# Expert token lists from the positions of maxima, and 16-row output products in four column groups

## The chip, the cores and the metric

The kernel runs on one core of one Trainium2 chip. The metric is the device time of one execution in microseconds (us), as the median of several. Engines are called PE (TensorE), PEld (its weight loads), DVE (VectorE), ACT (ScalarE), POOL (GpSimd) and SP (SyncE, which issues most transfers). Everything is computed in f32, where one matrix product is two records on PE.

## The reference, cut to what matters

Two hybrid attention layers on 512 tokens and 16 meta tokens, then a second block on 512 latent tokens and 256 context tokens with a neighbourhood-attention mixer and an RWKV mixer, each followed by an expert layer. The parts that the change touches:

```python
mixed = jnp.concatenate([o_a * silu(dz), o_b * silu(fz)], axis=-1)
return h + jnp.einsum('blm,md->bld', mixed, w_out)      # hybrid layer, 528 rows
...
cap = EC_CAPACITY * T // N_EXPERTS                       # 64 latent, 32 context tokens
aff = softmax(h @ w_router)                              # T x 16
gate, idx = lax.top_k(aff.T, cap)                        # each expert picks its tokens
xin = h[idx]
hid = silu(xin @ w1) * (xin @ w3)                        # 1024 x 1024 per expert
y = (hid @ w2) * gate[..., None]
return segment_sum(y, idx)
```

The order of the tokens within an expert's list doesn't matter, since the results are added back by index.

## The kernel before, in words

The program is a chain of stages. Each stage gives every engine its own list of instructions, joined by semaphores, and ends with a barrier of all engines. The weights come in chunks of 2 MB (2,097,152 bytes). `load_chunk` (line 92) issues one on SP's queue into a slot, `chunk_here` (106) makes PE wait for it. There are three slots (`ring`); in the last expert stage four more are made out of buffers that are free by then (`WIDE_SLOTS`, 7). A slot is loaded again when PE has finished with its chunk. So in the first expert stage SP's loads follow the semaphores `up` and `down` of PE with two chunks in flight or waiting while PE works on the third, and in the second stage with six.

**Output projection of a hybrid layer** (`hybrid_output`, line 934). A job is one tile of rows by one half of 512 columns. `begin` (line 957) multiplies the four blocks of the forget half, `end` (line 966) the four of the differential half, and DVE adds the bank onto X (line 1012). Tiles are four of 128 rows and, in layer 0 only, one of 16 meta rows. Six jobs begin ahead (j = 0 to 5, the first meta job is j = 4); the last job of all, j = 9, is the second meta job. In `hybrid_project` the 16 meta rows already are multiplied in four groups of 128 columns, each written to its own 32 partitions (lines 436 to 438).

**Routing** (`route`, line 1577). Affinities are turned to 16 rows (experts) by tokens in `left` (latent at partition 0, context at partition 32). Then eight turns of `max` (eight largest of each row, line 1672) and `match_replace` (those eight become -1, line 1673) mark the 64 chosen tokens of each expert (context rows take part in the first four turns). A compare, a running sum, a product and a subtraction (lines 1674 to 1677) give every chosen token its place in the list; PE turns these back to tokens by experts (1632), and DVE copies them to `slot` (1681). The stage ends there.

**Experts** (`experts`, line 1685). For every expert, DVE builds a one-hot matrix out of `slot` (`choose`, 1871 to 1874), PE multiplies it by pairs of (token number, affinity) (`place`, 1792), and DVE copies the result to the list of indices and gates (`list_tokens`, 1883 and 1884). Token numbers and the comparison row come from HBM as `moe_labels` (1728). POOL gathers the rows of the expert (`gather`, 1752), two experts ahead, and adds the results into HBM (`scatter`, 1761). PE's order for one expert is: four chunks of w1 and w3 (`rows_by`, 1782), `place` for the expert two ahead, the transposes of the hidden rows (`flip_hid`, 1805), the transposes of the next expert's gathered rows (`flip_xin`, 1798), two chunks of w2. DVE and ACT run their part in a loop of 4 by 4 experts (`Fori`), PE's is written out. The last turns list and gather an expert that doesn't exist (index 16). The first stage has both streams (64 + 32 rows, six tiles), the second only the latent one.

```python
for r in streams:
    last = rows_by(xinT[:, x % 2], w, j % 2, r, r.gates if j // 2 else r.ups)
last.then_inc(s.up, 1)
...
pe.wait_ge(s.onehot, e + 3)
place(x % 2)
for r in streams:
    pe.wait_ge(s.hid_ready, e * NS + r.at + 1)
    flip_hid(r)
pe.wait_ge(s.listed, e + 3)
...
flip_xin((x + 1) % 2)
```

Of the kernel before, what the change touches and what calls it, by code (L numbers as in the profile page):

```python
# [933 lines left out]
def hybrid_output(k, l, O, OT, Z, squares, blocks, uT, tiles, held):  # L934
# [5 lines left out]
    BANKS_OUT = 6  # L940
    with ExitStack() as mem, stage(k, "rooted inverted gated turned back product added mod_turned mod_back") as (block, s):
# [8 lines left out]
        def _(pe):  # L950
            def begin(j):
                n, t, rows = jobs[j]
                w = chunk_here(k, pe, c0 + n)
                if j >= BANKS_OUT:
                    pe.wait_ge(s.added, j - BANKS_OUT + 1)
                for a in range(half):
                    nc.tensor.matmul(bank(k, j % BANKS_OUT)[0:rows, :], OT(a)[:, t * P:t * P + rows], w[:, half + a, :],
                                     start=a == 0, stop=False)

            def end(j):  # L960
# [4 lines left out]
                for a in range(half):  # L965
                    last = nc.tensor.matmul(bank(k, j % BANKS_OUT)[0:rows, :], uT[:, a, t * P:t * P + rows], w[:, a, :],
                                            start=False, stop=a == half - 1)
# [32 lines left out]
        def _(dve):  # L1000
# [7 lines left out]
            def add(j):  # L1008
# [3 lines left out]
                nc.vector.tensor_tensor(x, x, bank(k, j % BANKS_OUT)[0:rows, :], ALU.add).then_inc(s.added, 1)  # L1012
# [544 lines left out]
ROUND = 4  # L1557
HALF_K = KD // 2
EPAD = EXPERTS + ROUND
# [17 lines left out]
def route(k, l, hT, xn, sums, aff, slot, tiles):  # L1577
# [8 lines left out]
    with ExitStack() as mem, stage(k, "parts copied logits exped turned placed step ready") as (block, s):  # L1586
        sb = lambda n, shape: mem.enter_context(nc.sbuf_tensor(f"{n}{k.stage_no}", shape, F32))
        stat = sb("stat", [P, 2, 8])
        left, rank, ones = sb("left", [rows, SEQ]), sb("rank", [rows, SEQ]), sb("ones", [rows, SEQ])
        part, pick = sb("part", [P, TOK2]), sb("pick", [P, 2, EXPERTS])  # L1590
        best = sb("best", [rows, 8])
# [17 lines left out]
        def _(pe):  # L1609
# [24 lines left out]
            last.then_inc(s.placed, 1)  # L1634

        @block.scalar
        def _(act):
# [4 lines left out]
            act.wait_ge(s.step, 9)  # L1642
# [3 lines left out]
        def _(dve):  # L1646
# [19 lines left out]
            nc.vector.tensor_tensor(aff[:, 0:nt, 0:EXPERTS], raw[:, :, :], wide(stat[:, 1, 0:nt]), ALU.mult).then_inc(s.ready, 1)  # L1666
# [11 lines left out]
            dve.wait_ge(s.placed, 1)  # L1678
            for n, (_, first, width, _) in enumerate(streams):
                ts = slice(first // P, (first + width) // P)  # L1680
                chain(nc.vector.tensor_copy(slot[:, ts, 0:EXPERTS], bank(k, 5 + n, nt * EXPERTS)
                                            .rearrange("p (t e) -> p t e", t=nt)[:, ts, :]))
# [1543 lines left out]
```

## Time and profile before

| | us |
|---|---|
| median of 3 runs | 3560.84 (3553.47 to 3570.84) |
| the profiled execution | 3576.05 |
| its span, first to last instruction | 3574.3 |
| PE busy in the span | 3179.9 (89%) |
| DVE busy | 1522.1 (43%) |
| ACT busy | 828.7 (23%) |
| mean DMA rate over the span | 169 GB/s |
| share of transfers in the chain that ended last | 10% |

A row of the view by stretches gives the stretch in us from the span's start, its length, busy time of each engine with its number of instructions, the granted clock of PE (1 is full), the mean busy share of the 16 DMA engines and their rate. The stages that the change touches lie at 414 to 490 us (output projection of layer 0), 1467 to 2094 (first routing and experts) and 3027 to 3574 (second routing and experts).

### The profile page before, as it was taken

The page shows a single profiled execution, that of the slowest core. Times are in us where ns is not written, and L with a number is a line of the kernel's source. Part 1 is how long each engine was busy: PE and PEld are TensorE (multiplying, and loading weights), DVE is VectorE, ACT ScalarE, POOL GpSimd, SP SyncE. Part 2 cuts the span into 40 slices and gives each one's busy share as a digit, 9 for nine tenths or more (in the row PEclk, how much of TensorE's full clock was granted, in tenths as well). Part 3 has the DMA queues.
Part 4 walks back from the last instruction along what each step waited for, and adds up shares of the span by engine and source line. Part 5 has one row for each costly group of instructions (what it writes and reads, how often), then busy time and mean ns, then how long its engine had stood idle before and what let it go on. Part 6 is the DMA issues. An engine that isn't in the chain of part 4 may idle for free. (4 is left out here: it accounts for less than half of the span.)

```text
span 3574.3 us, 73074 instructions
## 1 busy us (share of the span) xinstructions
PE 3179.9 (89%) x32020; PEld 1830.5 (51%) x32020; DVE 1522.1 (43%) x3460; ACT 828.7 (23%) x1876; POOL 285.1 (8%) x307
## 2 busy tenths in 40 slices
PE   6998999989799999599999979998888878787777
PEld 5855658556344565344444435547788764322222
DVE  3574535645202483412122244137878863311111
ACT  2113410134201372100000010137666640000000
POOL 0001000000000120000000000001222230000000
PEclk9998999989899999799999989989999999899999
DMA  5564135720221111299999961100000033799998
GB/s 175 152 196 148 25 81 152 211 78 25 96 65 47 29 39 71 105 367 370 366 357 373 372 222 71 41 1 4 4 4 5 4 115 137 289 403 401 402 404 341
DMA packets 148488, 603.35 MB, mean 169 GB/s; under 512 B 17489, under 2 KB 20369, under 8 KB 131665
## 3 DMA queue, kind: packets, MB, share of 16 engines
q1 hardware_dynamic: 141840, 577.10, 43.9%
q0 software_dynamic: 6336, 21.63, 2.6%
q8 instruction: 253, 4.15, 0.5%
q14 instruction: 59, 0.48, 0.0%
HBM read 576.01 MB, written 28.97 MB: 169 GB/s over the span
## 5 line engine op out<-in xcount | busy, mean ns | idle before, releaser
L1782 PE MATMUL psum<-ring,big 128*32 128x256 f32 (+1 forms) x5280 | 692.8, 479 | 40.0 <-DMA ring<-moe_w 18.9
L1782 PEld LDWEIGHTS psum<-ring,big 128*32 128x32 f32 (+1 forms) x5280 | 242.3, 122 | 478.2 <-issue 383.3
L414 PE MATMUL psum<-h_uT,ring 128*128 128x264 f32 x1280 | 290.5, 387 | 0.0
L1920 DVE TENSOR_TENSOR big<-big,psum 128x512 f32<-128x512 f32 (+1 forms) x48 | 27.3, 597 | 613.0 <-PE psum L1782 613.0
L543 DVE SCALAR_TENSOR_TENSOR h_O<-h_O,cond_silu 128x512 f32<-128x512 f32 x336 | 226.8, 743 | 102.1 <-DMA h_O<-ada_w 102.1
L414 PEld LDWEIGHTS psum<-h_uT,ring 128*128 128x128 f32 x1280 | 242.0, 190 | 46.5 <-issue 5.8
L1782 PE MATMUL psum<-big 128*64 128x512 f32 x864 | 205.6, 622 | 54.7 <-DMA big<-moe_w 34.2
L1272 PE MATMUL psum<-ring,big 128*128 128x512 f32 x576 | 252.4, 598 | 1.7 <-PEq L56 1.7
L2391 PE MATMUL psum<-ring,gates 64*64 64x128 f32 (+1 forms) x5120 | 171.9, 253 | 11.5 <-issue 9.9
L1932 DVE SCALAR_TENSOR_TENSOR big<-psum,big,gates 64x512 f32<-64x512 f32 (+1 forms) x128 | 78.8, 615 | 241.4 <-PE psum L1782 240.0
L1272 PEld LDWEIGHTS psum<-ring,big 128*128 128x128 f32 x576 | 109.5, 192 | 135.3 <-issue 135.3
L434 PE MATMUL psum<-ring,h_uT 128*128 128x512 f32 x384 | 170.0, 600 | 0.0
L1782 PEld LDWEIGHTS psum<-big 128*64 128x64 f32 x864 | 62.0, 142 | 190.0 <-issue 128.2
L1859 ACT ACTIVATE big<-psum 128x512 f32<-128x512 f32 (+1 forms) x48 | 23.5, 524 | 579.2 <-PE psum L1782 579.2
L1058 PE MATMUL psum<-ring,big 128*128 128x512 f32 x320 | 139.5, 598 | 5.8 <-PEq L56 5.8
L2391 PEld LDWEIGHTS psum<-ring,gates 64*64 64x64 f32 x5120 | 134.8, 134 | 14.9 <-issue 13.7
L2739 DVE TENSOR_TENSOR ring<-ring,psum 64x256 f32<-64x256 f32 x288 | 120.9, 420 | 13.6 <-ACT ring L2576 7.8
L2391 PE MATMUL psum<-gates,ring 64*64 64x64 f32 x3840 | 88.3, 224 | 38.8 <-ACT ring L2576 34.0
L434 PEld LDWEIGHTS psum<-ring,h_uT 128*128 128x128 f32 x384 | 72.6, 191 | 91.3 <-issue 91.2
L2180 PE MATMUL psum<-big,ring 128*128 128x512 f32 (+1 forms) x336 | 110.5, 491 | 1.1 <-issue 1.1
L1752 POOL DMA_INDIRECT big<-rows,index x34 | 40.4, 1188 | 872.9 <-DVE big L1884 872.9
L1332 DVE TENSOR_REDUCE stat<-sq 128x8 f32<-128x512 f32 x24 | 16.5, 686 | 211.5 <-ACT sq L1311 211.5
(352 smaller groups left out, 4626.7 us busy)
## 6 DMA issues: line engine op xcount, KB each, us to landing
ring<-moe_w SPq DMA_DIRECT2D x138, 2048.0 KB, 9.8
big<-moe_w SPq DMA_DIRECT2D x54, 2048.0 KB, 32.9
h_O<-ada_w SPq DMA_DIRECT2D x192, 256.0 KB, 3.0
ring<-w_in SPq DMA_DIRECT2D x16, 2048.0 KB, 13.2
ring<-na_w_qkv SPq DMA_DIRECT2D x6, 2048.0 KB, 8.1
ring<-w_out SPq DMA_DIRECT2D x4, 2048.0 KB, 8.1
bias_rows<-na_table SPq DMA_DIRECT2D x16, 480.0 KB, 13.8
ring<-bias_rows SPq DMA_DIRECT2D x16, 360.0 KB, 3.0
```

The lines of the kernel that those rows point to most:

```text
L414: last = nc.tensor.matmul(bank(k, pair_bank(q) + h, NH), w[:, a, f * P:(f + 1) * P], uT[:, a, halves[h]], start=a == 0, stop=a == KD - 1)
L434: last = nc.tensor.matmul(bank(k, b), uT[:, a, t * P:(t + 1) * P], w[:, a, :], **st)
L543: nc.vector.scalar_tensor_tensor(into, ada(u), by, into, ALU.mult, ALU.add).then_inc(s.acc, 1)
L1058: last = nc.tensor.matmul(bank(k, j % BANKS)[0:rows, :], srcT[:, a, t * P:t * P + rows], w[:, a, :], start=a == 0, stop=a == KD - 1)
L1272: last = nc.tensor.matmul(bank(k, j % FIRST_BANKS), hT[:, a, t * P:(t + 1) * P], w[:, a, :], start=a == 0, stop=a == KD - 1)
L1752: nc.gpsimd.indirect_dma_start(xg[0:M, e % 2, :], None, k.rows[:, :], bass.IndirectOffsetOnAxis(ap=index[0:M, e % ROUND:e % ROUND + 1], ax ...
L1782: last = nc.tensor.matmul(bank(k, b, r.width)[q * r.n:(q + 1) * r.n, :], rowsT[:, half * HALF_K + n, r.first:r.first + r.n], w[:, n, q * r ...
L1920: nc.vector.tensor_tensor(hid[:, wide(r)], silu[:, wide(r)], bank(k, r.gates, r.width), ALU.mult).then_inc(s.hid_ready, 1)
L1932: last = nc.vector.scalar_tensor_tensor(y[r.first:r.first + r.n, x % 2, cols], bank(k, r.downs, r.width)[mine, :], gate[mine, x, 2 * r.at ...
L2180: last = nc.tensor.matmul(bank(k, job_bank(j), n), w[:, a, at:at + P], xs[m][:, a, first:first + n], **st)
L2391: last = nc.tensor.matmul(bank(k, b, width, at + p % QUAD * width)[to:to + CH, :], lhs(lo, p), rhs(lo, p), start=start and n == 0, stop=st ...
L2739: last = tt(new[there], old[here], got[there, 1, :, :], ALU.add)
```

## The change

- `hybrid_output`: the two meta jobs are multiplied in four column groups of 128, each in its own 32 partitions of the bank, and added by four DVE instructions of 128 columns.
- `route`: every turn also asks for the positions of its eight maxima (`max_index`); the last `match_replace` goes. The positions, turned to f32 (context ones with 512 added), and the maxima themselves are the lists of tokens and gates; PE turns them from experts by places to places by experts, and DVE copies them to `index` and `gate` for all 16 experts at once. Compare, running sum, product, subtraction, `slot`, two memsets and the host's `moe_labels` go.
- `experts`: `choose`, `place`, `list_tokens`, `labels` and the loops go; all engines' lists are written out for 16 experts. POOL no longer waits for lists, and no expert 16 is gathered or flipped. In the first stage the gates of the latent stream are signalled ahead of the context's (`latent_gates`), the transposes are interleaved (hidden latent, first half of the gathered rows, hidden context, second half), and DVE waits for an older scatter ahead of the results.

The short name of the change also speaks of keys ahead of values. No hunk of the diff moves keys or values. The core of the diff:

```diff
 # hybrid_output
+                    if rows == P:
+                        nc.tensor.matmul(bank(k, j % BANKS_OUT), OT(a)[:, t * P:t * P + rows], w[:, half + a, :],
+                                         start=a == 0, stop=False)
+                        continue
+                    for m in range(PARTS):
+                        nc.tensor.matmul(part_rows(j % BANKS_OUT, m), OT(a)[:, t * P:t * P + rows], w[:, half + a, part_cols(m)],
+                                         start=a == 0, stop=False)
...
+                if rows == P:
+                    last = nc.vector.tensor_tensor(x, x, bank(k, j % BANKS_OUT), ALU.add)
+                for m in range(PARTS if rows < P else 0):
+                    last = nc.vector.tensor_tensor(x[:, part_cols(m)], x[:, part_cols(m)], part_rows(j % BANKS_OUT, m), ALU.add)
 # route, tensor
-            for t in range(nt):
-                lo, col = at(t)
-                last = nc.tensor.transpose(bank(k, 5 + (lo > 0), EXPERTS, t * EXPERTS), rank[lo:lo + EXPERTS, col:col + P],
-                                           k.ident[lo:lo + EXPERTS, lo:lo + EXPERTS])
+            for n, (lo, _, _, cap) in enumerate(streams):
+                eye = k.ident[lo:lo + EXPERTS, lo:lo + EXPERTS]
+                first = n * CAP_L
+                nc.tensor.matmul(bank(k, 5, EXPERTS)[first:first + cap, :], token[lo:lo + EXPERTS, 0:cap], eye, start=True, stop=True)
+                for q in range(P // cap):
+                    last = nc.tensor.matmul(bank(k, 6, EXPERTS, n * EXPERTS)[q * cap:(q + 1) * cap, :], best[lo:lo + EXPERTS, 0:cap], eye,
+                                            start=True, stop=True)
 # route, vector
-            chain(nc.vector.memset(slot[:, :, :], -1.0))
-            chain(nc.vector.memset(aff[:, :, :], 0.0))
...
-            chain(nc.vector.memset(ones[:, :], 1.0))
...
-                chain(nc.vector.max(best[0:high, :], left[0:high, :]))
-                chain(nc.vector.match_replace(left[0:high, :], best[0:high, :], left[0:high, :], -1.0))
-            chain(nc.vector.tensor_scalar(left[:, :], left[:, :], 0.0, None, ALU.is_lt))
-            chain(nc.vector.tensor_tensor_scan(rank[:, :], ones[:, :], left[:, :], 0.0, ALU.mult, ALU.add))
-            chain(nc.vector.tensor_tensor(rank[:, :], rank[:, :], left[:, :], ALU.mult))
-            nc.vector.tensor_scalar(rank[:, :], rank[:, :], -1.0, None, ALU.add).then_inc(s.ready, 1)
+                eight = slice(8 * n, 8 * n + 8)
+                chain(nc.vector.max(best[0:high, eight], left[0:high, :]))
+                chain(nc.vector.max_index(found[0:high, eight], best[0:high, eight], left[0:high, :]))
+                if n < CAP_L // 8 - 1:
+                    chain(nc.vector.match_replace(left[0:high, :], best[0:high, eight], left[0:high, :], -1.0))
+            for n, (lo, first, _, cap) in enumerate(streams):
+                mine = token[lo:lo + EXPERTS, 0:cap]
+                last = nc.vector.tensor_copy(mine, found[lo:lo + EXPERTS, 0:cap])
+                if first:
+                    chain(last)
+                    last = nc.vector.tensor_scalar(mine, mine, float(first), None, ALU.add)
+            last.then_inc(s.ready, 1)
+            dve.wait_ge(s.listed, 1)
...
+            nc.vector.tensor_copy(index[0:listed, :], bank(k, 5, EXPERTS)[0:listed, :])
+            nc.vector.tensor_copy(gate[:, 0:len(streams), :], bank(k, 6, len(streams) * EXPERTS).rearrange("p (n e) -> p n e", e=EXPERTS))
 # experts, gpsimd
-                pool.wait_ge(s.listed, e + 1)
...
-                if e + 2 <= EXPERTS:
+                if e + 2 < EXPERTS:
                     gather(e + 2)
 # experts, tensor
-                    pe.wait_ge(s.onehot, e + 3)
-                    place(x % 2)
...
+                        if j == 3 and r.at == 0 and NS > 1:
+                            last.then_inc(s.latent_gates, 1)
+                    last.then_inc(s.up, 1)
+                for r in streams:
+                    if NS == 1 and e + 1 < EXPERTS:
+                        flip_xin(e + 1, 0)
+                    pe.wait_ge(s.hid_ready, e * NS + r.at + 1)
+                    flip_hid(r)
+                    if NS > 1 and e + 1 < EXPERTS:
+                        flip_xin(e + 1, r.at)
+                if NS == 1 and e + 1 < EXPERTS:
+                    flip_xin(e + 1, 1)
 # experts, vector
+                    if r.at == 0 and NS > 1:
+                        dve.wait_ge(s.latent_gates, e + 1)
+                    else:
+                        dve.wait_ge(s.up, e * 4 + 4)
...
-                    list_tokens((x + 2) % ROUND)
-                    choose(e + 3, (x + 1) % 2)
...
+                if e >= 2:
+                    dve.wait_ge(s.scattered, 16 * (e - 1))
```

## Rows read from the trace of the kernel before

**Rows 1.** The view by stretches: output projection, first expert stage, second in two pieces.

```profile
430.00:460.00 30.00, 29.65 (x83) 11.77 (x82) 6.04 (x10) 0.00 (x0) 0.00 (x0) 1.00 0.01 1
...
1511.00:2090.00 579.00, 577.88 (x4983) 238.94 (x4984) 128.60 (x348) 33.04 (x68) 39.53 (x30) 0.99 0.95 362
...
3069.00:3130.00 61.00, 61.00 (x292) 22.86 (x294) 9.27 (x22) 2.99 (x5) 5.02 (x4) 0.97 0.91 356
3130.00:3535.00 405.00, 318.86 (x1450) 115.27 (x1446) 60.42 (x143) 18.78 (x28) 33.34 (x26) 0.96 1.02 402
```

**Rows 2.** Loads of the weights, issue to landing, first stage and then second.

```profile
DMA to landing us min/median/max: 7.1/9.6/12.0
...
DMA to landing us min/median/max: 7.5/32.9/36.0
```

**Rows 3.** Timeline, last meta job: start, length, engine, line; idle before in brackets.

```profile
482.90 3.61 PE L957 MATMUL psum<-ring,h_O 128*16 128x512 f32 x8
...
486.34 3.60 PE L966 MATMUL psum<-ring,h_uT 128*16 128x512 f32 x8
...
489.98 0.68 DVE L1012 TENSOR_TENSOR X<-X,psum 16x512 f32<-16x512 f32 x1 [6.28 <-PE psum L966]
```

**Rows 4.** Timeline of PE in the input projection: one meta job in four groups.

```profile
233.85 1.94 PE L437 MATMUL psum<-ring,h_uT 128*16 128x128 f32 x64
```

**Rows 5.** Timeline of the second routing: memset, first maxima, last replace, ranks, copy.

```profile
3033.43 0.48 DVE L1657 MEMSET ones<- 16x512 f32 x1 [0.16 <-DVE left L1656]
...
3039.55 0.68 DVE L1672 MAX8 best<-left 16x8 f32<-16x512 f32 x1
...
3050.71 0.08 DVE L1673 MATCH_VALUE_LOAD left<-best,left 16x8 f32 x1
...
3051.49 0.41 DVE L1674 TENSOR_SCALAR left<-left 16x512 f32<-16x512 f32 x1
3051.93 1.21 DVE L1675 TENSOR_TENSOR_SCAN rank<-ones,left 16x512 f32<-16x512 f32 x1
...
3055.00 0.23 DVE L1681 COPY slot<-psum 128x64 f32<-128x64 f32 x1 [0.69 <-PE psum L1632]
```

**Rows 6.** Timeline of PE, second routing: ranks turned back.

```profile
3054.36 0.60 PE L1632 MATMUL psum<-ident_sb,rank 16*128 16x16 f32 x4 [15.56 <-DVE rank L1677]
```

**Rows 7.** The chain that ended last, start of the second expert stage.

```profile
3056.15 2.09 DMA big<-moe_labels
...
3061.46 0.80 issue
3062.26 3.84 DMA big<-rows,index
```

**Rows 8.** Timeline, start of the first expert stage: labels issued, first gather.

```profile
1495.37 0.33 SPq L1728 DMA_DIRECT2D big<-moe_labels  x1
...
1502.93 1.12 POOL L1752 DMA_INDIRECT big<-rows,index  x1 [173.83 <-DVE big L1884]
```

**Rows 9.** Timeline of PE, first expert stage: one expert's pause, chunks, next pause.

```profile
1535.28 1.50 PE L1792 MATMUL psum<-big 128*128 128x2 f32 x12
...
1536.64 0.85 PE L1805 MATMUL psum<-ident_sb,big 128*128 128x128 f32 x6
...
1537.55 1.10 PE L1798 MATMUL psum<-ident_sb,big 96*128 96x96 f32 x8
...
1538.58 32.76 PE L1782 MATMUL psum<-ring,big 128*64 128x512 f32 x288
...
1571.27 1.50 PE L1792 MATMUL psum<-big 128*128 128x2 f32 x12
```

**Rows 10.** The view by stretches around two pauses; last columns are clock, DMA share, GB/s.

```profile
1715.00:1724.00 9.00, 9.00 (x84) 5.11 (x78) 4.81 (x16) 0.87 (x2) 1.21 (x1) 1.00 0.97 384
1751.00:1762.00 11.00, 10.94 (x80) 5.54 (x78) 4.81 (x16) 0.87 (x2) 1.21 (x1) 0.84 0.81 318
```

**Rows 11.** Timeline of PE, last weight chunk of the kernel.

```profile
3561.97 3.65 PE L1782 MATMUL psum<-big 128*64 128x512 f32 x16 [0.43 <-DMA big<-moe_w]
```

More of the change, by code:

```diff
@@ L965, in end @@
                 for a in range(half):
-                    last = nc.tensor.matmul(bank(k, j % BANKS_OUT)[0:rows, :], uT[:, a, t * P:t * P + rows], w[:, a, :],
-                                            start=False, stop=a == half - 1)
+                    ends = dict(start=False, stop=a == half - 1)
+                    if rows == P:
+                        last = nc.tensor.matmul(bank(k, j % BANKS_OUT), uT[:, a, t * P:t * P + rows], w[:, a, :], **ends)
+                        continue
+                    for m in range(PARTS):
+                        last = nc.tensor.matmul(part_rows(j % BANKS_OUT, m), uT[:, a, t * P:t * P + rows], w[:, a, part_cols(m)], **ends)
                 last.then_inc(s.product, 1)
@@ L1574, with route @@
 GROUP = 32
-def route(k, l, hT, xn, sums, aff, slot, tiles):
+def route(k, l, hT, xn, sums, index, gate, tiles):
     nc = k.nc
@@ L1585, in route @@
     rows = streams[-1][0] + EXPERTS
-    with ExitStack() as mem, stage(k, "parts copied logits exped turned placed step ready") as (block, s):
+    with ExitStack() as mem, stage(k, "parts copied logits exped turned listed step ready") as (block, s):
         sb = lambda n, shape: mem.enter_context(nc.sbuf_tensor(f"{n}{k.stage_no}", shape, F32))
         stat = sb("stat", [P, 2, 8])
-        left, rank, ones = sb("left", [rows, SEQ]), sb("rank", [rows, SEQ]), sb("ones", [rows, SEQ])
+        left, aff = sb("left", [rows, SEQ]), sb("aff", [P, nt, EXPERTS])
         part, pick = sb("part", [P, TOK2]), sb("pick", [P, 2, EXPERTS])
-        best = sb("best", [rows, 8])
+        best, token = sb("best", [rows, CAP_L]), sb("token", [rows, CAP_L])
+        found = mem.enter_context(nc.sbuf_tensor(f"found{k.stage_no}", [rows, CAP_L], mybir.dt.uint32))
         raw = sb("raw", [P, nt, EXPERTS])
@@ L1727, in _ @@
         def _(sp):
-            sp.dma_start(labels, k.d["moe_labels"]).then_inc(s.labels_here, 16)
             for e in range(EXPERTS):
@@ L1851, in _ @@
         @block.scalar
         def _(act):
-            with act.Fori(0, EXPERTS // ROUND) as it:
-                for x in range(ROUND):
-                    e = it * ROUND + x
-                    act.wait_ge(s.up, e * 4 + 2)
+            for e in range(EXPERTS):
+                act.wait_ge(s.up, e * 4 + 2)
+                if e:
                     act.wait_ge(s.hid_ready, e * NS)
-                    for r in streams:
-                        nc.scalar.activation(silu[:, wide(r)], bank(k, r.ups, r.width), ACT.Silu).then_inc(s.silued, 1)
+                for r in streams:
+                    nc.scalar.activation(silu[:, wide(r)], bank(k, r.ups, r.width), ACT.Silu).then_inc(s.silued, 1)
+                if e:
@@ L1879, in list_tokens @@
-            def list_tokens(x):
-                for r in streams:
-                    rows = slice(r.first, r.first + r.n)
-                    nc.vector.tensor_copy(index[rows, x:x + 1], bank(k, 7, 1, INDEX_AT + 2 * r.at)[rows, :])
-                nc.vector.tensor_copy(gate[:, x, 0:2 * NS], bank(k, 7, 2 * NS, INDEX_AT)).then_inc(s.listed, 1)
             def modulate(part, b):
@@ L1900, in modulate @@
                 last.then_inc(s.xin_ready, 1)
[L1902 to L1911 removed]
             modulate(0, 0)
[L1913 to L1916 removed]
+            for e in range(EXPERTS):
+                if e:
@@ L1936, in experts @@
+                last.then_inc(s.y_ready, 1)
     k.c += EXPERTS * W_CHUNKS
```

188 lines of the change are left out of this document (67 added, 121 removed).

## Prediction

> **What bounds the kernel now.** I read the view by stretches first, then the loads' times, then the timelines around each place that the diff touches. In the output projection of layer 0 PE is busy 29.65 of 30 us, at full clock and with no DMA: PE sets the time there [rows 1]. In the first expert stage PE is busy 577.88 of 579 us, at clock 0.99; the DMA engines are busy 0.95 at 362 GB/s, so PE is the bound and DMA follows closely [rows 1]. The second expert stage is the opposite case: after 3130 PE is busy 318.86 of 405 us while the DMA share is 1.02 at 402 GB/s [rows 1], and a load takes a median of 32.9 us to land, against 9.6 in the first stage [rows 2], since six are queued. There, work taken off PE or DVE is worth nothing once the loads run without a break; only what lies before the first slot is freed, and after the last load, counts. Between these stages stand the routings, where DVE works alone on a serial chain [rows 5].
>
> **1. Meta jobs in four groups.** A meta job costs 482.90 to 486.34 for its forget half and as much again for the other, 3.44 x 2 = 6.88 us [rows 3]. The same product, eight blocks in four groups of 128 columns, took 1.94 us for 64 records in the input projection [rows 4]. Two jobs save 2 x (6.88 - 1.94) = 9.9 us, all on PE's path, since PE doesn't idle. The last job's addition is the stage's last work: one instruction of 0.68 us [rows 3] becomes four of 128 columns, put at 0.2 each, so +0.15. **Net -9.8** (ends -9 and -10.5). Everything behind it comes earlier by as much; SP's load after the last product moves along.
>
> **2. Routing.** Eight turns go from 3039.55 to 3051.49 [rows 5], 1.49 each. New is a `max_index` a turn, which the trace doesn't have. `match_replace` is nearest: a load of the eight values and one pass over the same 512 columns, 3050.71 to 3051.49, 0.78 us [rows 5]. I take 0.78. Ends: a pass as cheap as the compare (0.41) with its value load (0.08), 0.49; one as dear as the running sum (1.21) with it, 1.29 [rows 5]. So +8 x 0.78, less the last replace: **+5.5** a routing (ends +3.1 and +9.5).
> The Trainium skill (Vector Engine (DVE) Microarchitecture Reference, The match/index hardware and the swap-based sort pattern) gives both as a value load and one stream over the input on the same match hardware, the index pass with a drain of eight positions behind it; by that the price would be that of `match_replace` and a little more, and the upper end would fall away. No run here shows it yet.
>
> In the second routing, before: loop end 3051.49, slot copied 3055.23 [rows 5], labels issued 3056.15, gather's transfer 3062.26 [rows 7], 10.8 us in all. New after the loop: one conversion 0.2; six small PE records, as the four of 0.60 [rows 6], 0.6; two copies of some 0.2 [rows 5] 0.4; the barrier as before, 3056.15 - 3055.23 = 0.9; POOL's issue 0.8 [rows 7]. Sum 2.9, so -7.9. The memset that stands ahead of the softmax until 3033.91 goes [rows 5]: PE's logits were done earlier by 0.4. **Second routing: +5.5 - 7.9 - 0.4 = -2.8.** POOL's queue loses its waits for lists; gathers 0 and 1 go out together and the flip needs only the first. SP's queue loses one load, ahead of which nothing waits.
> In the first routing, labels to gather was 1502.93 - 1495.37 = 7.6 [rows 8] against 6.1 in the second [rows 7], so 1.5 more goes; two more conversions (0.4), ten more records (1.0 by [rows 6] shared out) come, and the memset was hidden there (0.4): **-2.5.**
>
> **3. First expert stage, per expert.** PE's period is 1571.27 - 1535.28 = 35.99 us: 32.7 in six chunks (5.45 each), 1.36 in `place`, 0.91 and 1.03 in the transposes [rows 9]. `place` goes: -1.36. Was it covering something? While it ran, DVE made the hidden rows. Now the latent part is signalled ahead of the context's last products (256 columns in four groups against 512 in two, a third of the chunk's 5.45, some 1.8 us), while DVE's product of 512 columns takes about 0.7, as its addition in [rows 3]; and the context part, half as wide, is made under the latent transposes and half of the next rows' (about 1 us). So I take no new wait. If that cover failed, one such product (0.7 us) would show per expert. ACT's copy of the latent part fits under the interleaved rest. DVE's new wait for the scatter of two experts before has its results and the next expert's hidden rows behind it; that scatter was issued more than one period of 36 us earlier. 15 x 1.36 + (1.36 + 1.03 for the last expert, which flips nobody) = **-22.8**.
> Can DMA keep up? The share 0.95 over 579 us, divided by the 1.02 of saturation [rows 1], is 539 us, 33.7 per expert; PE would need 34.6. A chunk must land within two chunk times, 10.9 us, after its slot is free; the median is 9.6, the longest 12.0 [rows 2]. The slack is thin, yet the sum holds it. Zero is the lower end of this saving; the upper end is 22.8.
>
> **4. Clock.** In one pause the granted clock over 11 us was 0.84, where at the pause before it stayed at 1.00 [rows 10]: 0.16 x 11 = 1.7 us at 1.2 instead of 2.4 GHz, which costs PE 1.7 us. Three of 16 pauses did so. What preceded each drop was `place` (two columns a product) and the transposes. With 1.9 us of pause instead of 3.3 I take two of three away: **-3.4** (ends 0 and -5.1).
>
> **5. Second expert stage.** DMA-bound, so the written-out lists and the shorter PE order cost or give nothing; routing's -2.8 shifts the first freed slot and with it all loads. At the end, the gather of expert 16 (64 rows of 4 KB, 0.26 MB, 0.65 us at 402 GB/s) goes; it shared the engines with the last chunk, for which PE waited 0.43 [rows 11]: **-0.5**. DVE's and ACT's instructions for twelve more experts must be fetched; both idle most of either stage, so nothing.
>
> **Sum:** 9.8 + 2.8 + 2.5 + 22.8 + 3.4 + 0.5 = 41.8 us. Against the profiled execution, 3576.05, that is 3534.3, a ratio of 0.9883. That execution lay 0.4% above the median of the runs, 3560.84; on the median the same ratio gives 3519.2, say **3519**.
>
> **Rivals.**
> *A, the ring gives half back.* PE waits for chunks in the first stage, since a gather and a scatter fall in the same two chunk times. For it: longest landing 12.0 [rows 2]. Against: 0.9 us of room per expert. Half of 22.8 lost: 3530. Chance 0.15; it shows as PE waits on ring.
> *B, the index pass costs 1.29.* 2 x 8 x 0.5 = 8 us more: 3527. Chance 0.09.
> *C, the groups don't overlap here.* 9.9 lost: 3529. Chance 0.02, as [rows 4] show the very form.
> *D, the first stage is already at its DMA limit.* Its 362 GB/s would be all that 96-row gathers, adds and three slots allow. Then points 3 and 4 give nothing and 41.8 - 26.2 = 15.6 is left: 3545. Against it stands 402 GB/s in the second stage [rows 1], but with seven slots and 64 rows. Chance 0.05.
> The Trainium skill (DMA: Bandwidth & Descriptors, Where 436 GB/s comes from) says that transfers between HBM and SBUF are bound by about 358 GB/s per core, which would be case D. This trace doesn't agree: 402 GB/s over 405 us [rows 1].
> *E, slower.* `max_index` runs far longer than any DVE pass here. It stands 16 times on a chain that nothing covers, and decides from 0.78 + 41.8/16 = 3.4 us a piece; at 5 us it adds 26 net: 3587. Nothing in the trace speaks for it. Chance 0.03.
> *That the change doesn't do what it says:* no hunk moves keys or values; nothing is counted for that, and no chance of its own hangs on it.
>
> **Numbers.** My sum has 0.66, A 0.15, B 0.09, C 0.02: together faster 0.92. About 0.5% (18 us) is what a measurement of this kernel can tell. D's 15.6 lies within it, so same 0.05; slower 0.03. Range: the best ends (9.8 + 0.7, routing 2 x 2.4 better, clock 1.7 better) give some 7 us more, and the median of few runs strays by some 6 of their 17 us spread: 3506. Upwards it takes in A, B and C alone, and A with B: 3519 + 11 + 8 = 3538, with a little stray 3541. It leaves out D and E and the tails.
>
> **What would show it.** Two meta jobs of about 1.8 us on PE; index passes near 0.66 us after a 0.08 value load; first gathers 2 to 3 us sooner after the loop's start; PE's period in the first expert stage at 34.6, six chunks of 5.45 with 1.94 between them and no idle before the hidden transposes; DMA share there near 0.98; clock drops gone or rarer; the second stage as long as before from its first product. I am wrong if PE idles on ring loads, if its pause is over 2.5 us, or if the index pass takes over 1.3 us.

## The result, and the profile after

The changed kernel took 3534.54 us (median of 5 runs, 3527.53 to 3544.49) against 3555.27 (3552.08 to 3570.84) for the kernel before in the same measurement: a ratio of 0.9935, interval 0.9906 to 0.9964. Timed again it took 3538.86 (6 runs, 3532.34 to 3542.62) against 3563.86 (11 runs): 0.9924, interval 0.9905 to 0.9943, or 20 to 34 us less. So it is faster, by less than 1%, and the 3519 forecast promised some 15 us too much (20 by the second timing); the time lies inside the range, near its upper end.

The profiled executions seem to agree with the forecast: 3576.05 before, 3531.58 after, 44.5 less. They don't. The table gives the length of each stage from its first instruction to the first of the next (the first and third columns take in the norm that follows, which nobody touched), and the last one to the end of its last scatter's issue; "rest" is what no hunk touches, worked out as the span (3574.3, 3556.0, 3529.8, 3538.0) less the five columns.

| kernel | output projection | first routing | first experts | second routing | second experts | rest |
|---|---|---|---|---|---|---|
| before | 89.0 | 27.9 | 629.0 | 28.3 | 512.7 | 2287.4 |
| before, profiled again | 87.8 | 27.9 | 628.8 | 28.3 | 515.1 | 2268.1 |
| after | 78.2 | 31.0 | 610.3 | 30.5 | 507.9 | 2271.9 |
| after, profiled again | 79.3 | 31.1 | 608.9 | 30.5 | 507.3 | 2280.9 |

The same kernel before differs from itself by 19 us in stages that nobody touched. In the five touched stages after has 1257.9 against 1286.9: 29 us less, which lies within the 20 to 34 of the timed runs. The stage columns repeat to 2.4 us or better, so from here on I read these.

**Meta jobs.** The timeline of PE and DVE after, last job of the output projection (start, length, engine, line, idle before in brackets), which answers to [rows 3]:

```profile
466.75 1.07 PE L966 MATMUL psum<-ring,h_O 128*16 128x128 f32 x32
467.64 1.06 PE L980 MATMUL psum<-ring,h_uT 128*16 128x128 f32 x32
468.76 1.16 DVE L1028 TENSOR_TENSOR X<-X,psum 16x128 f32<-16x128 f32 x4 [1.21 <-PE psum L980]
```

Both halves of the job together now take 468.70 - 466.75 = 1.95 us, against 6.88. The four small additions take 1.16 in place of 0.68.

**Routing.** The timeline of the second routing after, its seventh turn and the start of the eighth, then the copy of the list, the first gather and the first product, which answers to [rows 5 to 7]:

```profile
3011.05 0.68 DVE L1689 MAX8 best<-left 16x8 f32<-16x512 f32 x1
3011.77 0.08 DVE L1690 MATCH_VALUE_LOAD found<-best,left 16x8 f32 x1
3011.85 0.67 DVE L1690 FIND_INDEX8 found<-best,left 16x8 uint32<-16x512 f32 x1
3012.55 0.08 DVE L1692 MATCH_VALUE_LOAD left<-best,left 16x8 f32 x1
3012.63 0.66 DVE L1692 MATCH_REPLACE8 left<-best,left 16x512 f32<-16x512 f32 x1
3013.33 0.68 DVE L1689 MAX8 best<-left 16x8 f32<-16x512 f32 x1
...
3015.73 0.17 DVE L1702 CAST index<-psum 64x16 int32<-64x16 f32 x1 [0.72 <-PE psum L1651]
3017.40 0.98 POOL L1766 DMA_INDIRECT big<-rows,index  x1 [104.62 <-POOLq L56]
3024.00 8.51 PE L1796 MATMUL psum<-ring,big 128*64 128x512 f32 x32 [1.64 <-DVE big L1883]
```

A turn takes 3013.33 - 3011.05 = 2.28 us where it took 1.49. The index pass is one value load of 0.08 and one pass of 0.67, like the replace pass beside it (0.08 and 0.66). The Trainium skill (Vector Engine (DVE) Microarchitecture Reference, The match/index hardware and the swap-based sort pattern) gives both instructions the same stream over the input; the trace agrees, 0.67 against 0.66. The first gather is issued 20.0 us after the first turn's start (2997.39 to 3017.40) where it was 22.7 [rows 5, 7].

**First expert stage.** The view by stretches (columns as in [rows 1]), first for the first expert stage and then for the steady part of the second:

```profile
1484.00:2060.00 576.00, 547.49 (x4816) 214.97 (x4812) 107.25 (x248) 29.25 (x64) 35.04 (x29) 0.99 0.99 369
...
3090.00:3490.00 400.00, 308.27 (x1320) 104.73 (x1316) 44.44 (x84) 14.33 (x24) 27.14 (x23) 0.94 1.02 401
```

PE now is busy 547.49 of 576 us, where before it was 577.88 of 579 [rows 1]. It idles, which was the forecast's own sign of error. Where, the timeline of PE shows, one expert's pause and what follows it (it answers to [rows 9]):

```profile
1503.63 0.66 PE L1814 MATMUL psum<-ident_sb,big 128*128 128x128 f32 x4
1504.12 0.58 PE L1806 MATMUL psum<-ident_sb,big 96*128 96x96 f32 x4
1504.54 0.38 PE L1814 MATMUL psum<-ident_sb,big 128*128 128x128 f32 x2
1504.76 0.58 PE L1806 MATMUL psum<-ident_sb,big 96*128 96x96 f32 x4
1505.27 27.31 PE L1796 MATMUL psum<-ring,big 128*64 128x512 f32 x240
1533.96 5.52 PE L1796 MATMUL psum<-ring,big 128*64 128x512 f32 x48 [1.38 <-DMA ring<-moe_w]
1539.40 0.66 PE L1814 MATMUL psum<-ident_sb,big 128*128 128x128 f32 x4
```

The pause is 1505.27 - 1503.63 = 1.64 us, less than the 1.94 forecast. But ahead of the sixth chunk, the last one before the next pause, PE waits 1.38 us for its weights. The groups of waits sum that up for this stage (us of waiting, how often, the longest), and the loads' times from issue to landing follow, which answer to the first line of [rows 2]:

```profile
PE psum L1796 <- DMA ring<-moe_w: 17.9, 13, 2.2
...
DMA to landing us min/median/max: 7.2/10.2/13.0
```

Thirteen waits of 1.4 us, one in each of the first thirteen periods and always at this chunk. The last two full periods have none:

```profile
1970.31 32.76 PE L1796 MATMUL psum<-ring,big 128*64 128x512 f32 x288
2004.64 32.76 PE L1796 MATMUL psum<-ring,big 128*64 128x512 f32 x288
```

They are also the two in which a scatter is issued but no gather any more, since the gather runs three experts ahead of the scatter before it and ends with expert 15. (Two more profiles with the same order, after again and the one with the old output projection, have four such periods: three without a wait, one 0.55 us too long.) The mean period over fifteen experts, from 1503.63 to the like record at 2037.33, is 35.58 us, where PE needs 6 x 5.45 + 1.63 = 34.33; before it was 36.31.

Which transfers are behind it? The timelines of POOL, first of the kernel before and then of after:

```profile
1538.15 1.04 POOL L1752 DMA_INDIRECT big<-rows,index  x1 [31.53 <-DVE big L1884]
1553.39 1.46 POOL L1761 DMA_INDIRECT sums<-big,index  x1 [14.19 <-DVE big L1932]
1573.58 1.22 POOL L1752 DMA_INDIRECT big<-rows,index  x1 [18.73 <-DVE big L1884]
```

```profile
1555.85 1.44 POOL L1775 DMA_INDIRECT sums<-big,index  x1 [33.08 <-DVE big L1907]
1557.60 0.93 POOL L1766 DMA_INDIRECT big<-rows,index  x1 [0.30 <-issue]
```

Before, POOL waited for the list of expert e+2 (`listed`), which DVE finished in PE's pause: the gather went out at 1538, as the pause ended, and the scatter 15 us later. After, no wait of its own holds the gather; it goes out as soon as POOL's queue has issued the scatter, which waits for an expert's results: some 16 us after the pause. Both fall on the flight of the same loads. This was the first theory, and the runs below test it.

### The profile page after: what moved, and what is told of

The parts are those of the page before. It is cut to its first block and busy times, and to the rows that moved or that the text cites. A ratio compares the mean times of both kernels' runs of the same rounds, so it can differ in the third digit from the quotient of the medians.

```text
span 3529.8 us, 71984 instructions
## 1 busy us (share of the span) xinstructions
PE 3107.2 (88%) x31752; PEld 1780.5 (50%) x31752; DVE 1477.4 (42%) x3284; ACT 822.0 (23%) x1870; POOL 274.8 (8%) x305
## 5 line engine op out<-in xcount | busy, mean ns | idle before, releaser
L1796 PE MATMUL psum<-ring,big 128*32 128x256 f32 (+1 forms) x5280 | 685.7, 476 | 62.0 <-DMA ring<-moe_w 48.7
L1796 PE MATMUL psum<-big 128*64 128x512 f32 x864 | 210.4, 635 | 56.9 <-DMA big<-moe_w 44.5
L1907 DVE SCALAR_TENSOR_TENSOR big<-psum,gate,gates 64x512 f32<-64x512 f32 (+1 forms) x128 | 78.7, 615 | 250.1 <-PE psum L1796 248.7
L1859 ACT ACTIVATE big<-psum 128x512 f32<-128x512 f32 (+1 forms) x48 | 23.5, 524 | 625.4 <-PE psum L1796 625.4
L2366 PEld LDWEIGHTS psum<-ring,gates 64*64 64x64 f32 x5120 | 134.4, 133 | 13.7 <-issue 12.2
L1866 ACT ACTIVATE big<-psum 128x512 f32<-128x512 f32 (+1 forms) x48 | 24.8, 526 | 389.1 <-PE psum L1814 389.1
L2366 PE MATMUL psum<-big,ring 64*64 64x64 f32 (+1 forms) x2816 | 106.8, 241 | 0.0
## 6 DMA issues: line engine op xcount, KB each, us to landing
ring<-moe_w SPq DMA_DIRECT2D x138, 2048.0 KB, 11.6
```

The lines of the kernel that those rows point to most:

```text
L1796: last = nc.tensor.matmul(bank(k, b, r.width)[q * r.n:(q + 1) * r.n, :], rowsT[:, half * HALF_K + n, r.first:r.first + r.n], w[:, n, q * r ...
L1907: last = nc.vector.scalar_tensor_tensor(y[r.first:r.first + r.n, e % 2, cols], bank(k, r.downs, r.width)[mine, :], gate[mine, r.at, e:e + ...
L2366: last = nc.tensor.matmul(bank(k, b, width, at + p % QUAD * width)[to:to + CH, :], lhs(lo, p), rhs(lo, p), start=start and n == 0, stop=st ...
```

## The experiments

All edits but those named "before" are made to the changed kernel. Beside each, the kernel before ran too, on the same chip; its time stands in brackets. A time without a number of runs is one run's, so the argument goes by the stage, the period and the waits.

### Only the gather put back into the pause

```diff
-                    pool.wait_ge(s.xin_flipped, e - 1)
+                    pool.wait_ge(s.xin_flipped, e if with_ctx else e - 1)
```

> The changed kernel with one edit: in the first expert stage a gather waits for the flip of the expert before its own, so that it leaves in PE's pause again instead of straight behind a scatter. Theory 1 (collision: scatter and gather together delay the one chunk that has two chunk times to land): the PE waits of 1.3 to 2.1 us per expert at the fourth chunk go, PE's period in the first expert stage falls from 35.7 to 34.4 to 34.8 us, the stage is 12 to 20 us shorter than in the changed kernel. Theory 2 (the stage is at its DMA rate): the waits move to another chunk, period 35.5 or more, stage the same within 3 us.

Measured: 3507.44 us (before 3559.41); timed over six runs below, it is 3526.96. The first expert stage fell from 610.3 to 597.0 us, the period from 35.58 to 34.71. The groups of waits, and the stretch that answers to the first one shown of after:

```profile
PE psum L1796 <- DMA ring<-moe_w: 2.3, 4, 0.9
```

```profile
1480.00:2037.00 557.00, 547.30 (x4816) 215.84 (x4812) 107.28 (x248) 29.25 (x64) 35.05 (x30) 1.00 1.00 380
```

The waits fell from 17.9 to 2.3 us (with 2.4 more at four chunk starts that the profile puts down to issue), and the DMA engines moved 380 GB/s where they had moved 369. In the timeline of POOL the order is that of before again, the gather in the pause and the scatter 14.5 us later:

```profile
1604.55 0.93 POOL L1766 DMA_INDIRECT big<-rows,index  x1 [18.36 <-PE psum L1806]
1619.09 1.44 POOL L1775 DMA_INDIRECT sums<-big,index  x1 [13.61 <-DVE big L1907]
```

### A longer pause, nothing else

Six small products that nobody reads stand at the head of each pause.

```diff
+                if with_ctx:
+                    for n in range(6):
+                        nc.tensor.matmul(bank(k, 7, 2, HALF_K * M), k.ident[:, :], k.router[:, l, 0, 0:2], start=n == 0, stop=n == 5)
```

> The changed kernel with twelve more PE records of two columns (some 1.4 us, their result unused) ahead of the transposes of every expert of the first stage. Theory 1 (collision, not rate): the wait at the fourth chunk stays at 1.3 us or more, since it hangs on that chunk's own flight, and the period grows to about 37 us, the stage by 15 to 22 us. Theory 2 (DMA rate): the added PE time is taken out of the waits, period stays at 35.6 to 36.0, stage the same within 4 us.

Measured: 3546.9 us (before 3559.41), pause 2.98 against 1.64, so +1.34, and period 36.75, so +1.17. The timeline of PE, two periods:

```profile
1614.57 5.52 PE L1796 MATMUL psum<-ring,big 128*64 128x512 f32 x48 [1.48 <-DMA ring<-moe_w]
1620.02 1.50 PE L1835 MATMUL psum<-router_sb,ident_sb 128*128 128x2 f32 x12
...
1651.88 5.52 PE L1796 MATMUL psum<-ring,big 128*64 128x512 f32 x48 [1.57 <-DMA ring<-moe_w]
1657.33 1.50 PE L1835 MATMUL psum<-router_sb,ident_sb 128*128 128x2 f32 x12
```

Had the DMA rate set the period, the pause's extra time would have been taken from the wait. It nearly all came on top: thirteen waits again, 15.3 us where it was 17.9, so 1.2 each against 1.4. So the wait hangs for the most part on where the transfers stand in the period, not on how long it is. Case D of the prediction falls here.

### The kernel before, with the gather behind the scatter

The edit turns the order round in both expert stages; the first is read.

```diff
+                scatter(e)
                 if e + 2 <= EXPERTS:
                     gather(e + 2)
-                scatter(e)
```

> The kernel before, with POOL's order turned round: scatter of an expert first, then the gather two ahead, so that the gather leaves straight behind the scatter as in the changed kernel. Theory 1 (collision): loads issued after the first chunk of an expert take 12 us or more instead of 9.8, PE waits for ring 1 to 2 us per expert, period up from 36.0 to 37.0 to 37.5, first expert stage 12 to 25 us longer than before. Theory 2 (DMA rate): PE needs 36.0 us per expert, more than the rate wants, so no waits and the same stage within 3 us.

Measured: 3583.71 us (before 3559.41), first expert stage 643.4, 14.4 more than before. The waits of PE, and then POOL's pair:

```profile
PE psum L1782 <- DMA ring<-moe_w: 16.9, 15, 1.7
```

```profile
1617.64 1.44 POOL L1761 DMA_INDIRECT sums<-big,index  x1 [34.68 <-DVE big L1932]
1619.38 0.92 POOL L1752 DMA_INDIRECT big<-rows,index  x1 [0.30 <-issue]
```

The old kernel gets the new wait by this swap alone, with its old pause of 3.3 us: the period is 37.28 against 36.31, though the clock fell once in this profile and three times in that of before, which hides 3.4 us of the stage's loss. That closes the case from the other side.

### Two more slots

The first expert stage gets five slots; the two new ones lie in buffers that are free by then. The core of the edit:

```diff
-        depth = SLOTS if with_ctx else WIDE_SLOTS
+        depth = 5 if with_ctx else WIDE_SLOTS
...
+            if k.c == k.moe0:
+                sp.wait_ge(s.parts, len(streams))
+                load_chunk(k, sp, k.c + SLOTS)
+                sp.wait_ge(k.rows_stored, k.n_stored + 16 * nt)
+                load_chunk(k, sp, k.c + SLOTS + 1)
```

> The changed kernel with five weight slots instead of three in the first expert stage (two buffers that are free there), gathers as in the changed kernel. Theory 1 (collision delays one chunk by 2 to 3 us, rate is enough): four chunks are queued, waits go, period 34.4 to 34.7, stage 15 to 20 us shorter. Theory 2 (DMA rate): DMA share 1.0 or more, period stays at 35.5 or more.

Measured: 3507.72 us (before 3559.41), first expert stage 589.9, period 34.33, which is PE's own need, and no wait on the ring. The gather is still where after has it, 0.3 us behind the scatter (timeline of POOL), and a load takes longer, which no longer matters with four in flight:

```profile
1627.64 1.44 POOL L1787 DMA_INDIRECT sums<-big,index  x1 [31.66 <-DVE big L1919]
1629.38 0.93 POOL L1778 DMA_INDIRECT big<-rows,index  x1 [0.30 <-issue]
```

```profile
DMA to landing us min/median/max: 8.4/12.2/14.6
```

From 1500 to 2030 us the DMA engines moved 384 GB/s here, against 375 in after over the same stretch. So they could carry the whole forecast rate. With three slots it was lack of slack, not of bandwidth.

### After again, gather late, and gather late with five slots, timed

> The changed kernel as it is, timed again in alternation with the kernel before, to narrow the interval. By the stage lengths of the two profiles (output projection -10.8, first routing and experts -15.6, second -2.6, without the stages that nothing touches): 29 us, ratio 0.992. By the full difference of the two profiled executions: 44 us, ratio 0.988.

> The changed kernel with the gathers of the first stage moved back into PE's pause. Theory 1 (collision): the 13 us that its first expert stage was shorter come out of the time: 42 us under the kernel before, ratio 0.988, 13 under the changed kernel. If it was noise between executions: the same as the changed kernel.

> Both remedies: gathers in PE's pause and five weight slots in the first stage. Theory 1: after either remedy PE is the bound (34.3 us a period with five slots, its six chunks of 5.45 and 1.64 of transposes), so the second adds nothing to the first: first expert stage 587 to 592 us, as with five slots alone, 7 under late gathers alone by the chunks issued ahead; ratio 0.985 to 0.988. If queueing still cost something with five slots: period under 34.2, which PE's products don't allow.

| kernel | us (runs) | ratio to before, interval | first experts |
|---|---|---|---|
| after | 3538.86 (6) | 0.9924, 0.9905 to 0.9943 | 608.9 |
| gather in the pause | 3526.96 (6) | 0.9889, 0.9868 to 0.9910 | 595.6 |
| the same with five slots | 3518.02 (5) | 0.9855, 0.9832 to 0.9878 | 590.0 |

After comes out at the 0.992 that the stage lengths gave, and not at the 0.988 of the two profiled executions. The intervals of the first two rows touch, but no run of the second (3513.32 to 3530.28) is as slow as the fastest of the first (3532.34). The last one is the best version found. It has what the forecast had promised, 3519, but by an edit that the change lacks. The medians put it 8.9 us ahead of the gather alone, though both the ratios' intervals and the runs overlap; the stage says 5.6 less, of which six waits on the ring were 3.0.

### The old output projection in the changed kernel

`hybrid_output` is as before, all else as after (the edit is the first hunk of the diff, taken back).

> The changed kernel with the old output projection, 16 meta rows by 512 columns in one piece. If the four groups overlap as in the input projection, the output projection of layer 0 is 9.5 to 10.5 us longer than in the changed kernel and everything behind it unchanged; if the saving was noise of that stage, the same within 2 us.

Measured: 3541.23 us (before 3563.86, median of 11), output projection 88.1 against 78.2 and 79.3 in the two profiles of after: 9.9 or 8.8 us for the groups. The timeline of PE shows the old pair again:

```profile
472.22 3.61 PE L957 MATMUL psum<-ring,h_O 128*16 128x512 f32 x8
475.67 3.60 PE L966 MATMUL psum<-ring,h_uT 128*16 128x512 f32 x8
```

### The scatter late, the gather left

POOL holds the scatter of an expert back until the next pause (it waits for `up` of the next expert's fourth chunk); the gather keeps its place.

```diff
+                for e in range(EXPERTS + 1):
+                    if e:
+                        pool.wait_ge(s.y_ready, e)
+                    if e + 2 < EXPERTS:
+                        gather(e + 2)
+                    if e:
+                        if e < EXPERTS:
+                            pool.wait_ge(s.up, 4 * e + 4)
+                        scatter(e - 1)
```

> The changed kernel, with the gathers of the first stage where they are (just behind the finished rows of an expert) and the scatter put off to PE's next pause instead. If the harm is that both fall into the flight of one chunk, either one moved away cures it: period 34.4 to 34.9, waits for ring under 0.4 us per expert. If the gather by itself does the harm at that place: period stays at 35.4 or more.

Measured: 3526.78 us (before 3561.98), but first experts 611.1 and period 35.69: nothing gained there. The timeline of PE:

```profile
1641.96 21.86 PE L1806 MATMUL psum<-ring,big 128*64 128x512 f32 x192
...
1665.05 5.52 PE L1806 MATMUL psum<-ring,big 128*64 128x512 f32 x48 [1.23 <-DMA ring<-moe_w]
...
1671.06 5.52 PE L1806 MATMUL psum<-ring,big 128*64 128x512 f32 x48 [0.49 <-DMA ring<-moe_w]
```

The waits are 16.8 us in 19 pieces, and they have moved: in place of one at the sixth chunk stand two here, at the fifth and the sixth. Apart from each other, the two transfers still cost 35.69 - 34.33 = 1.4 us a period (0.1 of it is a drop of the clock). So the first theory, that it is enough to keep them apart, fell: scatter first and gather 15 us behind it is no better than both at once. Nor is it the scatter in the pause by itself: the last two periods, without a gather, take 34.3 us here too.

The longest wait is followed by that drop of the clock. It begins 1.1 us after PE has started again, and two chunks take 12.66 us instead of 10.97:

```profile
1775.51 12.66 PE L1806 MATMUL psum<-ring,big 128*64 128x512 f32 x96 [3.68 <-DMA ring<-moe_w]
```

### The kernel before once more

> The kernel before once more, for how often the clock falls in the pauses of the first expert stage and how much the stages that nobody touches wander. If the three drops of the profiled execution belong to the pause of 3.3 us: two to five drops again. If they are chance: none or one, and the first expert stage some 3 to 5 us shorter (624 to 626).

Measured: 3557.81 us, 18 us under the first profiled execution of the same kernel, with the expert stages the same to 2.4 us (table in the first section). In the view by stretches the clock falls again around a pause, here the one that starts at 1734.07, as in [rows 10], where the pause before it shows none:

```profile
1698.00:1709.00 11.00, 11.00 (x91) 5.72 (x86) 4.81 (x16) 0.87 (x2) 1.21 (x1) 1.00 0.93 348
1734.00:1745.00 11.00, 10.94 (x80) 5.54 (x78) 4.81 (x16) 0.87 (x2) 1.21 (x1) 0.84 0.82 316
```

### Both transfers in the pause

Gather and scatter are both held until the next pause.

```diff
+                    if e:
+                        if e < EXPERTS:
+                            pool.wait_ge(s.up, 4 * e + 4)
+                        scatter(e - 1)
+                    if e + 2 < EXPERTS:
+                        gather(e + 2)
```

> The changed kernel with scatter and gather of the first stage both in PE's pause, one right behind the other. If what counts is only how much slack the chunk in flight has (the one issued ahead of the pause has 7.1 + 5.4 = 12.5 us to land, the one after the first chunk of an expert 10.9): waits small, period 34.3 to 34.8, exp stage like with late gathers (595 to 600 us). If two indirect transfers close together harm wherever they are: period 35.3 or more, waits behind the pause.

Measured: 3520.98 us (before 3554.27), first experts 604.7, period 35.28. The groups of waits of PE:

```profile
PE psum L1804 <- DMA ring<-moe_w: 9.8, 11, 1.6
```

Here the wait stands at the fourth chunk after the pause, 1.12 us in the period that starts at 1643.30, and 3.4 us more in five pieces at chunk starts are put down to issue. Of the excess of 1.25 us a period 0.95 is left: in the pause too, two transfers at once do harm. The load that is issued behind the first chunk after the pause, while both are in flight, took a median of 11.8 us, where in after it took 7.8; and it is the one that the fourth chunk waits for.

### A scatter of 16 rows

POOL adds only the first 16 of an expert's 96 rows; the results of the other 80 are left out.

```diff
+                m = 16 if with_ctx else M
-                                             y[0:M, e % 2, :], None, compute_op=ALU.add).then_inc(s.scattered, 16)
+                                             y[0:m, e % 2, :], None, compute_op=ALU.add).then_inc(s.scattered, 16)
```

> The changed kernel, whose scatter in the first stage adds only 16 of 96 rows (80 rows of every expert are left out of the sum), gathers just behind it as in the changed kernel. If the harm needs the traffic of both: the chunk in flight lands 1 to 1.5 us sooner, waits under 0.4 us per expert, period 34.4 to 34.8. If the gather alone does it at that place: waits of 1 us or more stay, period 35.3 or more.

Measured: 3515.72 us (before 3554.27), first experts 594.6, period 34.62. The waits of PE, with the gather at after's place (it follows the scatter by 0.3 us):

```profile
PE psum L1797 <- DMA ring<-moe_w: 3.8, 6, 0.9
```

So the gather by itself does little harm there; it needs the scatter's 96 rows as well. The two last periods of after show the reverse, the full scatter at its place and no gather, without a wait. What decides in after is therefore what both together put beside one load's flight, and not that POOL issues two in a row.

The flight of that one load shows it directly. It is issued behind an expert's first chunk and has two chunk times, 10.9 us, to land. The median of its landing times, in each profile with three slots that records them:

| kernel | the critical load, us | waits on the ring, us |
|---|---|---|
| before | 9.9 | 0 |
| before, gather behind the scatter | 11.9 | 16.9 |
| after | 12.1 | 17.9 |
| the old output projection in the changed kernel | 11.9 | 17.0 |
| after, the two periods without a gather | 10.2 and 10.5 | 0 |
| gather in the pause (the timed one) | 10.7 | 3.0 |
| scatter of 16 rows | 10.6 | 3.8 |

The link holds period by period. In all sixty periods of the four changed kernels in the table, the period is 34.33 us plus what this load takes beyond 10.7 us, to within 0.2 us; it is 35.78 after a landing of 12.2, and 34.33 after one of 10.5.

## Why the prediction was half right

Measured is the change's own part, 29 us in the five touched stages, against a sum of 41.8. The time fell into the range because the range took in case A. That the sum is only 13 us off is in part luck: waits of 19 us that it put at nothing stand against some 7 us that PE's pauses, the clock and the routings gave beyond it.

- **Point 1, meta jobs, -9.8:** held. 89.0 to 78.2 in the first pair of profiles, 87.8 to 79.3 in the second, 8.8 and 9.9 by taking the part back.
- **Point 2, routings, -2.5 and -2.8:** held; they gave a little more. From the stage's first instruction to the first expert product it was 43.87, then 40.56 us in the first, and 41.16, then 37.84 in the second: -3.3 each. (The other profiles of the changed kernel with its edits, whose routing is the same, have 40.1 to 40.5 and 36.2 to 38.1, so the second varies by 2 us.) The price of a turn was right, 0.79 against 0.78, so case B falls. The routing columns themselves grew by 3.1 and 2.2, since the turns stand there; the gain lies at the start of the next stage, where labels and first lists went.
- **Point 3, first expert stage, -22.8:** the saving was real, and was given back in part. From the first expert product to the stage's end it was 613.05 us and is 600.73: -12.3 (the other 6.4 of the column's 18.7 are the routing's). The terms: fifteen pauses of 1.64 instead of 3.28 and a last one of 1.45 instead of 3.31, -26.5 where I had 22.8; the clock's three drops, -5.1; and the ring's waits, 15 x (35.58 - 34.33) = +18.8. That adds up to -12.8; the rest lies ahead of the first pause and behind the last chunk. (The waits listed by the profile are 17.9 of the 18.8.)
- **The step that failed** is the one in point 2, "POOL's queue loses its waits for lists; gathers 0 and 1 go out together": I saw there what the removed wait did at the stage's start, and not that it also held gather e+2 in PE's pause for the rest of the stage. With it went the step in point 3, "The slack is thin, yet the sum holds it": it was a sum of bytes by time, and a ring of three slots asks for one landing within 10.9 us, not for an average. The load that is issued behind an expert's first chunk took a median of 9.9 us before and takes 12.1 after; that is 1.4 beyond the 10.7 from which on PE waits, and PE waited 1.4. The 12.0 that I held against the 10.9 [rows 2] was another load, the one issued in a pause, which had the pause as well, some 14 us. Case A, which had chance 0.15, is what happened: PE's waits on the ring were its sign, and 19 us its cost where I had put 11.
- **Point 4, the clock, -3.4:** three drops of 3.4 us at the ends of pauses before, each half lost (1.7 us), none after, so -5.1. The reason given, a shorter pause without `place`, is neither shown nor refuted. For it: the three profiles of kernels with `place` have 3, 3 and 1 drops at 16 pauses, the ten with the short pause none at a pause (the one drop of the late scatter follows a wait of 3.68 us). Against it: the kernel with the filler has a pause of 3.0 us, again with two-column products, and no drop; but that is one profile. What decides stays open.
- **Point 5, the second stage, -0.5:** the column went from 512.7 (515.1 in the second profile) to 507.9, but nearly all of that is the routing's. From its first product to the end the stage took 499.9 (502.3) and takes 500.5, so it is as long as before, as forecast, and 0.5 is below what the same kernel varies. Nor did the last chunk gain, for which PE waited 0.43 before and waits 0.48:

```profile
3517.57 3.65 PE L1796 MATMUL psum<-big 128*64 128x512 f32 x16 [0.48 <-DMA big<-moe_w]
```

- **Case D, a DMA limit in the first stage,** falls by the filler (waits stay while the period grows) and by five slots (34.33 us a period). The Trainium skill (DMA: Bandwidth & Descriptors, Where 436 GB/s comes from) puts the bound between HBM and SBUF at about 358 GB/s per core. This case doesn't agree: 380 GB/s over 557 us with the gather in the pause, 401 over 400 us in the second stage after. **Case C** falls by the meta jobs, **case E** by the 0.67 us pass.

Left open: why a scatter in the pause with the gather 16 us behind it costs as much as both together, while the mirror of it costs nearly nothing. The bytes are the same. The two don't weigh alike in the pause: with the late gather a gather there took a median of 4.7 us to land (8.5 in the kernel before), with the late scatter a scatter there took 11.1. And in the latter kernel the load behind the second chunk after the pause took 11.6 (up to 14.6), where in after it took 8.0; the fifth chunk waits for it. Why is a guess, and a run with the scatter's place moved in steps, which could tell, wasn't made.

## What to carry to other kernels

A wait that is removed because its reason is gone may also have been what spaced two transfers. Before it goes, list what stands behind it in its queue, say at which point of the period each transfer will now start, and hold the landing time of the load in flight there against what the ring allows for one load; a mean share of the DMA engines doesn't answer that. With two loads in flight, tie such transfers to a point of the consumer's order by a wait of their own, or make the ring deeper, which makes their place irrelevant. And when a change is worth 1%, compare stages between two profiles: the untouched ones differed by 19 us.

## What was unexpected of the hardware

- **The share of busy DMA engines is only a rough measure of work.** The same stage ran at share 0.99 and 369 GB/s after, and at 1.00 and 380 GB/s with the gather in the pause; before it was 0.95 at 362 [rows 1]. Divided by its share, a stretch moved 381 GB/s before, 373 after, 380 with the gather in the pause and 393 in the second stage after, so the bytes that a busy engine stands for differ by 5%. That is more than my estimate had left (33.7 us of DMA work against a period of 34.6, 3%), so the division by the saturated share of 1.02 was no bound. That it could keep up was true, by five slots, but not by that sum.
- **The order of two small transfers is worth 13 us.** One gather of 96 rows per expert, 16 us sooner or later in a period of 35 us, makes 2.3 or 17.9 us of waits, and 597.0 or 610.3 us of the stage; timed, the medians differ by 12 us.
- **Clock drops in short pauses** came three times in each of two profiles of before, at pauses 37.5 us apart (1754.6, 1792.2, 1829.7, then 1737.5, 1775.1, 1812.6), and not at the other thirteen, whose instructions are the same. They are the same three in both, the seventh, eighth and ninth of the stage, and the one drop of the kernel before with the swap is at the seventh too. So it hardly is chance which pause is hit, but no run here shows what picks it.
